# Delta rule: one of three modulation chunks as one-column products on TensorE, between the fills of the inverse's levels

## The chip, the core and the metric

One core of one Trainium2 chip. The metric is the time of one execution of the whole program on the device, in microseconds (us). The kernel before was run three times (2866.32, 2871.13 and 2872.02 us, median 2871.13); one more execution was recorded by the hardware profiler.

## What is computed

The reference is a stack of two transformer blocks at 256 tokens and a width of 2048. The change touches one stage of the first block, the gated delta rule, and a vector that this stage computes on the side:

```
mod = silu(c) @ w_ada + b_ada                       # 2048 x 12288, six parts of 2048 columns
...
m = strict_lower(beta * (k k^T) * gamma)            # per head and chunk of tokens
sol = triangular_solve(I + m, rhs)                  # u and w of the delta rule
v_new = u - w S ;  o = (q e^g) S + (q k^T * gamma) v_new ;  S = S * tail + k_tail^T v_new
```

`mod` is a product of a vector with a matrix of 2048 x 12288. Its weights are read once, in 24 chunks of 512 columns, and the chunks are spread as side work over several stages. The stage of the delta rule makes three of them (chunks 15, 16 and 17).

## The kernel before, in words

The stage is the function `phase_gdn`. All engines work at once, each in the order of its own code, and wait for each other by semaphores only. Eight heads are held in four quads of squares (n = 0 to 3), with 128 tokens to a square.

The triangular system is solved by building the inverse in levels. The code numbers them l = 0 to 5. In each level TensorE fills four banks `("p", l, n)` (8 products of 64x64 each), ScalarE copies each to `P1` (line 2127), TensorE fills four banks `("d", l, n)` (16 products of 64x64 each; the profile shows an f32 product as two records, so 16 records for a p and 32 for a d), and VectorE merges each into `T` and `UD` with two predicated copies (lines 2359 and 2361). The fill p of quad n of the next level waits until VectorE has merged d of quad n. TensorE has one queue: it makes p of the four quads, then d of the four quads, in this order. All fills are recorded at line 2164. The last level (l = 5) is half as large. Level 0 is followed by four `qk` banks.

After the last level VectorE copies the squares to `U` (lines 2381 and 2384), and TensorE goes on with the state products `vn0`, `s`, `ks`, `vn1` and the outputs. ScalarE's last steps (a logarithm, the load of a table, an exponential) end the stage.

The side work is the class `Ada`: POOL loads 512 KB of `w_ada` at a time (two rows of tiles of 128x512, line 233) into a ring of four slots, and VectorE multiplies each tile by one number per partition and adds it up (line 274 for the first two steps of a chunk, line 278 for the rest). Sixteen steps make a chunk, and three more operations reduce it (lines 283, 289 and 292); TensorE sums the rest over partitions after the outputs (line 191), and VectorE adds the bias (line 179). VectorE's code places the steps by two tables: `LEVEL_STEPS` says how many steps follow the merge of each quad in levels 0 to 4, and two more numbers how many stand before the keys and the outputs. What is left is done after the outputs.

SyncE issues nothing in this stage. `gdn_work` is a buffer of five parts; its last, `BB`, is free from the last `strict_products` of VectorE until ScalarE squares the outputs into it.

One-column products with weights as the stationary operand exist elsewhere in the program: in the setup stage `ada_group` makes two chunks so (line 344).

Of the kernel before, what the change touches and what calls it, by code (L numbers as in the profile page):

```python
# [14 lines left out]
P = 128  # L15
# [3 lines left out]
KT = D // P  # L19
# [7 lines left out]
CW = 512  # L27
NT = CW // P
# [132 lines left out]
AK = 2  # L161
# [3 lines left out]
AGROUPS = KT // AK  # L165
ADA_BANK = 7


def ada_column(which, chunk):

    return NMOD * which + NT * chunk


def add_bias(nc, core, which, chunk, chunks, bank=ADA_BANK):

    at, n = NT * chunk, NT * chunks
    bias = (C_BADA, C_BADA2)[which] + at
    sums = ada_column(which, chunk)
    return nc.vector.tensor_tensor(core.mod[:, which, at:at + n], core.ps[:, bank, sums:sums + n],
                                   core.cols[:, bias:bias + n], ALU.add)  # L180
# [1276 lines left out]
            next(program, None)  # L1457


GDN_CHUNKS = (15, 16, 17)  # L1460
LEVEL_STEPS = (2, 2, 2, 2, 2)
STEPS_BEFORE_KEYS, STEPS_BEFORE_OUTPUTS = 5, 2


AFTER_REFILL = {2: (2, 3), 3: (4,), 4: (5,), 5: (6, 7), 6: (8,), 7: (9,)}
# [538 lines left out]
def phase_gdn(nc, core, w_ada):  # L2004


    big, ps = core.big, core.ps
# [4 lines left out]
    NI = len(inv_levels)  # L2012
# [14 lines left out]
    with ExitStack() as ctx:  # L2027
# [3 lines left out]
        sem = lambda n: ctx.enter_context(nc.semaphore(n))  # L2031
        silu_ready, eg_ready, \
            g1_ready, g1_exp, nt_ready, tu_ready, r0_ready, eg_bc, qd_ready, sq_ready, \
            rs_ready, r1_ready, qkm_ready, cleared = (sem(n) for n in (
                "silu_gg_ready", "eg_ready", "g1_ready", "g1_exp", "nt_ready", "tu_ready", "r0_ready",
                "eg_bc", "qd_ready", "sq_ready", "rs_ready", "r1_ready", "qkm_ready", "inverse_cleared"))
        W = ctx.enter_context(nc.sbuf_tensor("gdn_work", [P, 5, HH * SEQ], F32))
        G1, QK, NT_, GB, BB = (W[:, n, :] for n in range(5))
        rows = ctx.enter_context(nc.sbuf_tensor("gdn_rows", [HH, 2, SEQ], F32))
# [13 lines left out]
        ident_square = ctx.enter_context(nc.sbuf_tensor("ident_square", [P, HP], F32))  # L2053
        ada = Ada(ctx, nc, core, [(w_ada, 0, chunk, 1) for chunk in GDN_CHUNKS], 1)
        block = ctx.enter_context(nc.Block())
# [5 lines left out]
        as_blocks = lambda a: a.rearrange("p (n t) -> p n t", t=P)  # L2061

        made = {}

        @block.gpsimd
        def _(pool):
# [8 lines left out]
            for n in reversed(range(1, len(LEVELS))):  # L2075
# [7 lines left out]
                if n in (4, 2):  # L2083
                    for load in range(4 + (4 - n), 6 + (4 - n)):
                        ada.load_when_free(pool, 0, load)
            for load in range(8, len(GDN_CHUNKS) * AGROUPS):
                ada.load_when_free(pool, 0, load)
# [71 lines left out]
        def _(pe):  # L2159
            def fill(name, parts):  # L2160

                banks.wait_empty(pe, name)
                for out, lhsT, rhs, start, stop in parts:
                    ins = nc.tensor.matmul(out, lhsT, rhs, start=start, stop=stop)
                ins.then_inc(banks.filled, 1)
# [20 lines left out]
            for j, (of, r, c) in enumerate(((gates, 0, 0), (gates, 0, 1), (gates, 1, 0), (gates, 1, 1), (rows, 0, 1),  # L2186
                                            (rows, 1, 0))):
                ins = nc.tensor.transpose(ps[:, banks.bank("columns"), j * HH:(j + 1) * HH],
                                          of[:, r, c * P:(c + 1) * P], core.ident[0:HH, 0:HH])
# [7 lines left out]
            def in_quad(n):  # L2197
                return [(j, 4 * n + j) for j in range(4)]

            for half in range(2):  # L2200
                for n in range(2 * half, 2 * half + 2):
                    pe.wait_ge(nt_ready, n + 1)
                    fill(("nt", n), [(half_ps(("nt", n), 0)[e, j, :], NTb[e, m, e], core.ident[e, e], True, True)
                                     for j, m in in_quad(n) for e in EDGES])
                for n in range(2 * half, 2 * half + 2):
                    fill_turned(("v", n), [big[:, GV + 2 * n + j // 2, (j % 2) * P:(j % 2 + 1) * P] for j in range(4)])
            for n in range(2):
                fill_turned(("kt", n), [big[:, GK + 4 * n + j, 0:P] for j in range(4)])
            for l in range(NI):
                for n in range(4):  # L2210
                    if l == 0:
                        pe.wait_ge(tu_ready, n + 1)
                    else:
                        pe.wait_ge(banks.emptied["dve"], n_dve[("d", l - 1, n)])
                    p = half_ps(("p", l, n), 0)
                    if l < NI - 1:
                        fill(("p", l, n), [(p[e, j, :], NTb[e, m, e], T[e, m, :], True, True)
                                           for j, m in in_quad(n) for e in EDGES])
                    else:
                        fill(("p", l, n), [(p[LOW, j, :], NTb[TOP, m, LOW], T[TOP, m, :], True, True)  # L2220
                                           for j, m in in_quad(n)])
                for n in range(4):
                    pe.wait_ge(banks.emptied["act"], n_act[("p", l, n)])
                    d, dt = half_ps(("d", l, n), 0), half_ps(("d", l, n), 1)
                    if l < NI - 1:
                        fill(("d", l, n), [(d[e, j, :], UD[e, m, :], P1[e, m, :], True, True)
                                           for j, m in in_quad(n) for e in EDGES]
                             + [(dt[e, j, :], P1[e, m, :], UD[e, m, :], True, True)
                                for j, m in in_quad(n) for e in EDGES])
                    else:  # L2230
                        fill(("d", l, n), [(dt[TOP, j, :], P1[LOW, m, :], UD[LOW, m, :], True, True)
                                           for j, m in in_quad(n)])
                if l == 0:
                    fill_products("qk", q_all, 0, 4)
# [38 lines left out]
        def _(dve):  # L2273
# [34 lines left out]
            def columns_of(a, L, high):  # L2308
                return a.rearrange("p n (b two l) -> p n b two l", two=2, l=L)[:, :, :, high, :]
# [27 lines left out]
            for n in range(4):  # L2337
# [3 lines left out]
                for edge in EDGES:  # L2341
                    ins = nc.vector.copy_predicated(columns_of(quad(UD, n)[edge], 1, 1),
                                                    mask_of(up_square, last, 1, 1, edge),
                                                    columns_of(quad(NTb, n)[edge, :, edge], 1, 1))
# [9 lines left out]
            for l, L in enumerate(inv_levels[:-1]):  # L2354
                m = LEVELS.index(L)
                dve.wait_ge(core.pool.sem, made[m])
                for n in range(4):
# [5 lines left out]
                                              ).then_inc(banks.emptied["dve"], 1)  # L2363
                    sum_steps(LEVEL_STEPS[l])
                if l == 0:
# [22 lines left out]
            for n in range(2):  # L2388
                banks.wait_filled(dve, ("ks", n))
                for j in range(4):  # L2390
                    h = 4 * n + j
                    ins = nc.vector.scalar_tensor_tensor(out=value(1, h), in0=quad_ps(("ks", n))[:, j, :],
                                                         scalar=pc[:, 6, h:h + 1], in1=value(1, h),
                                                         op0=ALU.mult, op1=ALU.add)
# [7 lines left out]
            for n, at in enumerate(quarters):  # L2402
# [3 lines left out]
                    in1=flat(GG, HH)[:, at], op0=ALU.mult, op1=ALU.mult).then_inc(banks.emptied["dve"], 1)  # L2406
            sum_steps(KT * len(GDN_CHUNKS) - done)
            for n, at in enumerate(quarters):
# [2 lines left out]
                v.mark(nc.vector.tensor_tensor(o[:, at], o[:, at], GB[:, at], ALU.mult))  # L2411
            dve.wait_ge(v.sem, v.n)
            ada.add_biases(dve)

# [1089 lines left out]
```

## Time and profile before

| | us |
|---|---|
| median of three runs | 2871.13 (2866.32 to 2872.02) |
| profiled execution, time | 2862.77 |
| its span, first to last instruction | 2861.0 |
| the stage of the delta rule in it | 556.4 to about 655.4 |
| levels 1 to 4 on TensorE | 589.15 to about 622 |

Times in the trace count from the first instruction. An engine's busy time in a window counts what it does, not whether anybody waits for it. PEclk, the granted clock, is 1.00 at 2.4 GHz and 0.50 at 1.2 GHz.

### The profile page before, as it was taken

The page shows a single profiled execution, that of the slowest core. Times are in us where ns is not written, and L with a number is a line of the kernel's source. Part 1 is how long each engine was busy: PE and PEld are TensorE (multiplying, and loading weights), DVE is VectorE, ACT ScalarE, POOL GpSimd, SP SyncE. Part 2 cuts the span into 40 slices and gives each one's busy share as a digit, 9 for nine tenths or more (in the row PEclk, how much of TensorE's full clock was granted, in tenths as well). Part 3 has the DMA queues.
Part 4 walks back from the last instruction along what each step waited for, and adds up shares of the span by engine and source line. Part 5 has one row for each costly group of instructions (what it writes and reads, how often), then busy time and mean ns, then how long its engine had stood idle before and what let it go on. Part 6 is the DMA issues. An engine that isn't in the chain of part 4 may idle for free. (4 is left out here: it accounts for less than half of the span.)

```text
span 2861.0 us, 50952 instructions
## 1 busy us (share of the span) xinstructions
PE 2726.7 (95%) x19637; PEld 2514.4 (88%) x19637; DVE 2038.9 (71%) x2921; ACT 1369.9 (48%) x2222; POOL 462.9 (16%) x592
## 2 busy tenths in 40 slices
PE   8799999988999999999998999998999999999998
PEld 8789999877878888999998988887878888889998
DVE  6768996786877777777877588785587655555554
ACT  1355446545455555445444454555344444444454
POOL 1002998121011111111110022220011000000000
PEclk7799999989999999999999999999999999999999
DMA  9756666546487887887883776664568655665563
GB/s 386 253 202 234 220 228 202 196 149 221 153 283 270 279 276 267 272 275 267 283 279 87 204 230 231 215 221 136 162 242 292 224 182 184 190 191 161 178 190 127
DMA packets 290940, 632.48 MB, mean 221 GB/s; under 512 B 31490, under 2 KB 52422, under 8 KB 290502
## 3 DMA queue, kind: packets, MB, share of 16 engines
q1 hardware_dynamic: 239120, 484.78, 51.0%
q0 software_dynamic: 40192, 142.63, 14.7%
q10 hardware_dynamic: 11446, 2.54, 0.6%
q8 instruction: 127, 2.08, 0.3%
q14 instruction: 55, 0.45, 0.0%
HBM read 627.77 MB, written 2.10 MB: 220 GB/s over the span
## 5 line engine op out<-in xcount | busy, mean ns | idle before, releaser
L1188 DVE TENSOR_TENSOR weight_parts<-weights,weight_parts 128x1024 fp32r<-128x1024 f32 x584 | 705.9, 1220 | 298.5 <-ACT weight_parts L1109 297.9
L1109 ACT ACTIVATE weight_parts<-weights 128x1024 fp32r<-128x1024 f32 x584 | 606.4, 1056 | 556.4 <-PE accumulators L1298 245.3
L1287 PE MATMUL accumulators<-h_parts,weight_parts 128*128 128x512 f32 x2816 | 780.7, 399 | 19.8 <-DVE h_parts L1175 8.5
L1287 PEld LDWEIGHTS accumulators<-h_parts,weight_parts 128*128 128x128 f32 x2816 | 487.3, 191 | 90.1 <-DVE h_parts L848 9.4
L1298 PEld LDWEIGHTS accumulators<-h_parts,weight_parts 128*128 128x128 f32 x2944 | 454.1, 191 | 68.5 <-DVE weight_parts L1188 7.5
L1298 PE MATMUL accumulators<-h_parts,weight_parts 128*128 128x256 f32 x2944 | 473.6, 283 | 5.6 <-DVE weight_parts L1188 5.6
L1333 PE MATMUL accumulators<-h_parts,weight_parts 128*128 128x256 f32 x1728 | 436.1, 284 | 1.8 <-DVE weight_parts L1188 1.8
L1335 PE MATMUL accumulators<-h_parts,weight_parts 128*128 128x256 f32 x1728 | 435.6, 284 | 0.0
L1333 PEld LDWEIGHTS accumulators<-h_parts,weight_parts 128*128 128x128 f32 x1728 | 333.9, 193 | 2.3 <-DVE weight_parts L1188 2.3
L1335 PEld LDWEIGHTS accumulators<-h_parts,weight_parts 128*128 128x128 f32 x1728 | 333.8, 193 | 0.0
L1329 PE MATMUL accumulators<-h_parts,weight_parts 128*128 128x256 f32 x1728 | 279.9, 285 | 8.9 <-ACT weight_parts L1109 8.9
L1655 PE MATMUL accumulators<-in_h_parts,in_weight_parts 128*128 128x256 f32 x1024 | 263.2, 289 | 13.9 <-DVE in_weight_parts L1976 13.6
L1657 PE MATMUL accumulators<-in_h_parts,in_weight_parts 128*128 128x256 f32 x1024 | 260.0, 286 | 0.0
L1815 ACT ACTIVATE in_weight_parts<-weights 128x512 fp32r<-128x512 f32 x256 | 157.2, 630 | 201.8 <-PE accumulators L1657 147.8
L1329 PEld LDWEIGHTS accumulators<-h_parts,weight_parts 128*128 128x128 f32 x1728 | 240.1, 193 | 9.3 <-ACT weight_parts L1109 9.3
L1976 DVE TENSOR_TENSOR in_weight_parts<-weights,in_weight_parts 128x512 fp32r<-128x512 f32 x256 | 188.4, 748 | 77.0 <-ACT in_weight_parts L1815 76.6
L2884 PE MATMUL accumulators<-in_h_parts,in_weight_parts 128*128 128x256 f32 x1632 | 216.8, 287 | 9.7 <-DVE in_weight_parts L3269 4.1
L2884 PEld LDWEIGHTS accumulators<-in_h_parts,in_weight_parts 128*128 128x128 f32 x1632 | 203.3, 192 | 21.0 <-issue 8.4
L1655 PEld LDWEIGHTS accumulators<-in_h_parts,in_weight_parts 128*128 128x128 f32 x1024 | 199.0, 194 | 19.0 <-DVE in_weight_parts L1976 18.7
L1657 PEld LDWEIGHTS accumulators<-in_h_parts,in_weight_parts 128*128 128x128 f32 x1024 | 199.3, 195 | 0.0
L3020 ACT ACTIVATE in_weight_parts<-weights 128x512 fp32r<-128x512 f32 (+6 forms) x224 | 120.8, 554 | 153.8 <-PE accumulators L2884 146.0
L1648 PE MATMUL accumulators<-in_h_parts,in_weight_parts 128*128 128x256 f32 x1024 | 177.0, 296 | 3.7 <-DVE in_h_parts L1846 3.7
(409 smaller groups left out, 3373.3 us busy)
## 6 DMA issues: line engine op xcount, KB each, us to landing
weights<-in_w_ff SPq DMA_DIRECT2D x256, 512.0 KB, 5.5
weights<-in_w_in SPq DMA_DIRECT2D x160, 512.0 KB, 5.0
h_t<-in_ada_w POOLq DMA_DIRECT2D x96, 512.0 KB, 6.6
weights<-in_ffn_w_gate SPq DMA_DIRECT2D x88, 512.0 KB, 4.6
weights<-in_ffn_w_up SPq DMA_DIRECT2D x88, 512.0 KB, 4.6
weights<-in_ffn_w_down SPq DMA_DIRECT2D x88, 512.0 KB, 4.2
weights<-in_w_out SPq DMA_DIRECT2D x64, 512.0 KB, 4.6
wide<-in_ada_w POOLq DMA_DIRECT2D x128, 256.0 KB, 3.8
```

The source lines that it names most:

```text
L1109: nc.scalar.activation(w[:, held:held + take, 0, :], core.ring[:, q % RING, k:k + take, :], ACT.Copy).then_inc(core.high_ready, take)
L1188: ins = nc.vector.tensor_tensor(w[:, held:held + take, 1, :], core.ring[:, q % RING, k:k + take, :], w[:, held:held + take, 0, :].bitcast( ...
L1287: nc.tensor.matmul(core.ps[:, nt, :], high, x[:, kt].rearrange("p a t -> p (a t)"), start=(kt == 0), stop=False, skip_group_check=True)
L1298: ins = nc.tensor.matmul(rest(nt) if two else acc(c, nt), w[:, held, 1, nt * P:(nt + 1) * P], x[:, kt, 0, :], start=False, stop=(kt == KT ...
L1329: nc.tensor.matmul(accs[nt], w[:, held, 0, cols[nt]], xk[:, 0, :], start=(first and nt % 2 == 0), stop=False, skip_group_check=True)
L1333: nc.tensor.matmul(accs[nt], w[:, held, 0, cols[nt]], xk[:, 1, :], start=False, stop=False, skip_group_check=True)
L1335: ins = nc.tensor.matmul(accs[nt], w[:, held, 1, cols[nt]], xk[:, 0, :], start=False, stop=(last and nt % 2 == 1), skip_group_check=True)
L1648: nc.tensor.matmul(acc(c, nt), w[:, k, 0, nt * P:(nt + 1) * P], x[:, kt, 0, :], start=(kt == 0 and nt % 2 == 0), stop=False, skip_group_ch ...
L1655: nc.tensor.matmul(acc(c, nt), w[:, k, 0, nt * P:(nt + 1) * P], x[:, kt, 1, :], start=False, stop=False, skip_group_check=True)
L1657: ins = nc.tensor.matmul(acc(c, nt), w[:, k, 1, nt * P:(nt + 1) * P], x[:, kt, 0, :], start=False, stop=(kt == KT - 1 and nt % 2 == 1), sk ...
L1976: ins = nc.vector.tensor_tensor(w[:, k, 1, :], core.ring[:, g % RING, part, :], w[:, k, 0, :].bitcast(F32), ALU.subtract)
L2884: ins = nc.tensor.matmul(out, stationary[:, a], moving[:, b], start=(kt == 0 and i == 0 and j == 0), stop=(kt == KT - 1 and i == 2 and j = ...
```

## The change

Chunk 17 leaves VectorE. Its 16 rows of tiles become 64 one-column products on TensorE: the stationary operand is a 128x128 square of weights, the moving one a column of `c_act`, and the sums stay in one PSUM bank until VectorE adds the bias. Two products follow each p fill and each d fill of levels 1 to 4 (32 places with two products each). SyncE loads the weights in eight loads of 512 KB into two slots in `BB`; a load waits until TensorE has used up the slot, and TensorE waits for a load at every fourth place. VectorE's tables shrink from 48 steps to 32: one step instead of two behind each merge of levels 2 to 4, two instead of five before the keys, one instead of two before the outputs.

```diff
-GDN_CHUNKS = (15, 16, 17)
-LEVEL_STEPS = (2, 2, 2, 2, 2)
-STEPS_BEFORE_KEYS, STEPS_BEFORE_OUTPUTS = 5, 2
+GDN_CHUNKS, GDN_PE_CHUNK = (15, 16), 17
+LEVEL_STEPS = (2, 2, 1, 1, 1)
+STEPS_BEFORE_KEYS, STEPS_BEFORE_OUTPUTS = 2, 1
...
+        mod_ring = BB.rearrange("p (s k n) -> p s k n", s=2, k=AK)
+
+        @block.sync
+        def _(sp):
+            sp.wait_ge(nt_ready, 4)
+            for load in range(AGROUPS):
+                if load >= 2:
+                    sp.wait_ge(mod_used, load - 1)
+                sp.dma_start(mod_ring[:, load % 2], mod_columns[:, load]).then_inc(mod_landed[load % 2], 16)
...
+            def modulation(point):
+                kt = point // 2
+                load = kt // AK
+                if point % (2 * AK) == 0:
+                    pe.wait_ge(mod_landed[load % 2], 16 * (load // 2 + 1))
+                for j in (2 * (point % 2), 2 * (point % 2) + 1):
+                    ins = nc.tensor.matmul(ps[:, ADA_BANK, mod_at + j:mod_at + j + 1],
+                                           mod_ring[:, load % 2, kt % AK, j * P:(j + 1) * P], core.c_act[:, kt:kt + 1],
+                                           start=(kt == 0 and j == 0), stop=(kt == KT - 1 and j == NT - 1),
+                                           skip_group_check=True)
+                if point % (2 * AK) == 2 * AK - 1:
+                    ins.then_inc(mod_used, 1)
...
+                    if 1 <= l < NI - 1:
+                        modulation(8 * (l - 1) + n)
...
+                        if l:
+                            modulation(8 * (l - 1) + 4 + n)
...
             ada.add_biases(dve)
+            dve.wait_ge(mod_used, AGROUPS)
+            add_bias(nc, core, 0, GDN_PE_CHUNK, 1)
```

On TensorE, level 1 and the start of level 2 stood so before. Rows `wide,gdn_work 64x64` are p fills, rows `wide 64x64` are d fills, and x32 is four fills of 8 products:

```order
L2164 MATMUL accumulators<-wide 128x128 x16
L2164 MATMUL accumulators<-wide,gdn_work 64x64 x32
L2164 MATMUL accumulators<-wide 64x64 x64
L2164 MATMUL accumulators<-wide,gdn_work 64x64 x32
L2164 MATMUL accumulators<-wide 64x64 x64
```

With the change, a part of the same level reads so; line 2176 is the fills and line 2218 the new products:

```order
L2176 MATMUL accumulators<-wide 128x128 x16
L2176 MATMUL accumulators<-wide,gdn_work 64x64 x8
L2218 MATMUL accumulators<-c_act,gdn_work 128x1 x2
L2176 MATMUL accumulators<-wide,gdn_work 64x64 x8
L2218 MATMUL accumulators<-c_act,gdn_work 128x1 x2
L2176 MATMUL accumulators<-wide,gdn_work 64x64 x8
L2218 MATMUL accumulators<-c_act,gdn_work 128x1 x2
L2176 MATMUL accumulators<-wide,gdn_work 64x64 x8
L2218 MATMUL accumulators<-c_act,gdn_work 128x1 x2
L2176 MATMUL accumulators<-wide 64x64 x16
L2218 MATMUL accumulators<-c_act,gdn_work 128x1 x2
```

Each of the 32 fills of levels 1 to 4 is now followed by a pair of products with the whole array as its tile, and the next fill stands behind that pair.

On VectorE, the piece from the last quad of level 3 through level 4 to the copies of `U` stood so before (lines 2359 and 2361 are a merge, 274 and 278 the steps of the side work):

```order
L2359 COPY_PREDICATED wide<-low_square,accumulators 128x8x16
L2361 COPY_PREDICATED wide<-up_square,accumulators 128x8x16
L278 SCALAR_TENSOR_TENSOR ada_sums<-ada_weights,c_act,ada_sums 128x512 x2
L283 TENSOR_TENSOR ada_sums<-ada_sums 128x512
L289 STREAM_TRANSPOSE ada_sums<-ada_sums 128x512
L292 TENSOR_REDUCE ada_rows<-ada_sums 128x16
L2359 COPY_PREDICATED wide<-low_square,accumulators 128x4x32
L2361 COPY_PREDICATED wide<-up_square,accumulators 128x4x32
L274 TENSOR_SCALAR ada_sums<-ada_weights,c_act 128x512 x2
L2359 COPY_PREDICATED wide<-low_square,accumulators 128x4x32
L2361 COPY_PREDICATED wide<-up_square,accumulators 128x4x32
```

With the change the same piece is (lines 2388 and 2390 are the merge):

```order
L2388 COPY_PREDICATED wide<-low_square,accumulators 128x8x16
L2390 COPY_PREDICATED wide<-up_square,accumulators 128x8x16
L278 SCALAR_TENSOR_TENSOR ada_sums<-ada_weights,c_act,ada_sums 128x512
L2388 COPY_PREDICATED wide<-low_square,accumulators 128x4x32
L2390 COPY_PREDICATED wide<-up_square,accumulators 128x4x32
L278 SCALAR_TENSOR_TENSOR ada_sums<-ada_weights,c_act,ada_sums 128x512
```

One step stands where two stood, and the reduction of a chunk between levels 3 and 4 is gone; the second chunk is now reduced behind the outputs, where the third was.

## Rows read from the trace of the kernel before

**Rows 1.** The page: busy time, share of the span and instructions.

```profile
PE 2726.7 (95%) x19637; PEld 2514.4 (88%) x19637; DVE 2038.9 (71%) x2921; ACT 1369.9 (48%) x2222; POOL 462.9 (16%) x592
```

**Rows 2.** Stretch: length; busy of PE, PEld, DVE, ACT, POOL; PEclk, DMA share, GB/s.

```profile
596.00:606.00 10.00, 6.40 (x197) 5.86 (x194) 9.90 (x20) 4.84 (x16) 3.24 (x5) 1.00 0.64 219
```

**Rows 3.** Timeline of VectorE, levels 2 to 5: start, length, instruction, idle time before.

```profile
601.88 2.28 DVE L2370 TENSOR_TENSOR gdn_work<-gdn_work,incl 128x2048 f32<-128x2048 f32 x1
...
619.19 0.69 DVE L283 TENSOR_TENSOR ada_sums<-ada_sums 128x512 f32<-128x512 f32 x1
...
621.26 0.29 DVE L2359 COPY_PREDICATED wide<-low_square,accumulators 128x128 f32<-128x128 int32 x1
...
626.29 1.41 DVE L278 SCALAR_TENSOR_TENSOR ada_sums<-ada_weights,c_act,ada_sums 128x512 f32<-128x512 f32 x2
627.61 2.40 DVE L2381 COPY wide<-wide 64x256 f32<-64x256 f32 x8
630.03 1.41 DVE L2384 COPY wide<-accumulators 64x256 f32<-64x256 f32 x4
631.47 3.40 DVE L278 SCALAR_TENSOR_TENSOR ada_sums<-ada_weights,c_act,ada_sums 128x512 f32<-128x512 f32 x5
637.45 2.40 DVE L2392 SCALAR_TENSOR_TENSOR wide<-accumulators,gdn_token_cols,wide 128x128 f32<-128x128 f32 x8 [2.58 <-PE accumulators L2164]
```

**Rows 4.** Timeline of TensorE, levels 1 and 2, and the first state product.

```profile
589.15 2.48 PE L2164 MATMUL accumulators<-wide,gdn_work 64*64 64x64 f32 x64
591.55 3.95 PE L2164 MATMUL accumulators<-wide 64*64 64x64 f32 x128
...
596.79 0.68 PE L2164 MATMUL accumulators<-wide,gdn_work 64*64 64x64 f32 x16 [0.36 <-DVE wide L2361]
...
607.53 1.12 PE L2164 MATMUL accumulators<-wide,gdn_work 64*64 64x64 f32 x16 [1.04 <-DVE wide L2361]
...
626.95 2.73 PE L2164 MATMUL accumulators<-wide 64*64 64x64 f32 x29
630.88 5.57 PE L2164 MATMUL accumulators<-wide 128*128 128x128 f32 x32 [1.20 <-issue]
```

**Rows 5.** Timeline of TensorE, windows 576.3:577 and 578.7:579.3 (cut at their edges).

```profile
576.12 0.57 PE L2164 MATMUL accumulators<-ident,gdn_work 64*64 64x64 f32 x14
576.63 0.55 PE L2170 MATMUL accumulators<-ident,wide 128*128 128x128 f32 x3
...
578.51 0.60 PE L2170 MATMUL accumulators<-ident,wide 128*128 128x128 f32 x4
579.04 0.45 PE L2164 MATMUL accumulators<-wide,gdn_work 64*64 64x64 f32 x8
```

**Rows 6.** Two groups of records: duration ns min/median/max, first and last start.

```profile
L2164 PE MATMUL accumulators<-wide,gdn_work x368: 218/218/366, 579.0 to 646.0; 64*64 64x64 f32 x176, 128*128 128x128 f32 x8
...
L2170 PE MATMUL accumulators<-ident,wide x24: 272/273/330, 574.3 to 578.8; 128*128 128x128 f32 x24
```

**Rows 7.** Timeline of TensorE in the setup stage, one-column products.

```profile
35.66 3.63 PE L344 MATMUL accumulators<-c_act,weights 128*128 128x1 f32 x32
...
74.77 6.96 PE L344 MATMUL accumulators<-c_act,weights 128*128 128x1 f32 x32
```

**Rows 8.** TensorE by stretch: length, busy time (records), granted clock, DMA share, GB/s.

```profile
40.40:53.90 13.50, 13.50 (x66) 0.50 1.05 405
...
603.00:607.10 4.10, 1.36 (x32) 1.00 0.30 108
607.50:610.10 2.60, 1.97 (x32) 0.50 0.73 203
610.10:613.90 3.80, 3.80 (x78) 0.50 0.89 319
```

**Rows 9.** DMA issues in the window 583:630.

```profile
ada_weights<-in_w_ada POOLq DMA_DIRECT2D x20, 512.0 KB, 4.9
```

**Rows 10.** Timeline of VectorE, the stage's last operation.

```profile
655.21 0.17 DVE L179 TENSOR_TENSOR modulation<-accumulators,small_vectors 128x12 f32<-128x12 f32 x1
```

More of the change, by code:

```diff
@@ L2033, in phase_gdn @@
             g1_ready, g1_exp, nt_ready, tu_ready, r0_ready, eg_bc, qd_ready, sq_ready, \
-            rs_ready, r1_ready, qkm_ready, cleared = (sem(n) for n in (
+            rs_ready, r1_ready, qkm_ready, cleared, mod_used, *mod_landed = (sem(n) for n in (
                 "silu_gg_ready", "eg_ready", "g1_ready", "g1_exp", "nt_ready", "tu_ready", "r0_ready",
-                "eg_bc", "qd_ready", "sq_ready", "rs_ready", "r1_ready", "qkm_ready", "inverse_cleared"))
+                "eg_bc", "qd_ready", "sq_ready", "rs_ready", "r1_ready", "qkm_ready", "inverse_cleared", "pe_modulation_used",
+                "pe_modulation_landed_0", "pe_modulation_landed_1"))
+        mod_columns = w_ada.rearrange("(g k p) n -> p g k n", p=P, k=AK)[:, :, :, GDN_PE_CHUNK * CW:(GDN_PE_CHUNK + 1) * CW]
+        mod_at = ada_column(0, GDN_PE_CHUNK)
         W = ctx.enter_context(nc.sbuf_tensor("gdn_work", [P, 5, HH * SEQ], F32))
```

## The prediction, made before the kernel was run

> **What bounds the kernel now.** I read the page first: TensorE is busy for 95% of the span and VectorE for 71% [rows 1]. That is a mean over many stages and says little of a change that sits in one of them, the stage of the delta rule, about 100 us long. So I went to that stage's windows and timelines. In 596 to 606 VectorE is busy for 9.90 of 10 us and TensorE for 6.40 [rows 2]. The timelines show who ends whose wait: inside levels 1 to 4 TensorE's gaps before a p fill end with VectorE's merge at line 2361 (0.36 and 1.04 us in [rows 4]), while VectorE goes from one row into the next, through the mask of QK (2.28 us), the steps and the reduction of a chunk [rows 3]. VectorE therefore sets the pace of levels 1 to 4, with side work between the merges. TensorE starts level 1 at 589.15, and the first state product starts at 630.88 [rows 4], right after VectorE's copies to U at 627.61 and 630.03 [rows 3]. From there TensorE and ScalarE set the end: VectorE waits 2.58 us for TensorE although it still had five steps of side work to fill the time [rows 3]. The number to forecast is when the first state product starts; what lies behind it moves with it.
>
> **What is taken from VectorE.** Levels 2 to 4 lose 12 steps. Two steps take 1.41 us from first start to last end, but a step overlaps the next, so one is worth about 0.67 us (five take 3.40, [rows 3]): 8.0 us. The reduction of a chunk from 619.19 to the next merge at 621.26 also goes from the levels: 2.1 us. Together 10.1 us on the engine that bounds now. The three steps fewer before the keys (2 us) and the one fewer before the outputs stand ahead of waits and bring nothing: the 2.58 us only grow.
>
> **What TensorE gets.** 64 products, seen as two records each, are 128 records. Setup shows such records back to back: 32 in 3.63 us at the full clock, 0.113 us each, and 32 in 6.96 us at half, 0.22 each [rows 7]. That makes 14.3 us at full clock. But they come as 32 groups of four records between fills whose tile is 64x64, and each group changes the tile twice. The trace has such changes. The last 64x64 record before 576.63 starts at 576.12 + 0.57 - 0.22 = 576.47, so entering costs 0.16 us; the third record of the 128x128 run starts 0.55 - 0.27 = 0.28 us after the first, the fourth 0.11 later, 0.39 in all; the way back is from 578.51 + 0.60 - 0.27 = 578.84 to 579.04, 0.20 us [rows 5, 6]. A group of four thus puts 0.16 + 0.39 + 0.20 = 0.75 us between two fills instead of 4 x 0.113 = 0.45. Those rows have 128 moving columns or few, mine have one; I take 0.75 and keep 0.45 as the lower bound, and for the upper the doubled figure at half clock. The Trainium skill ("TensorEngine Tiling (Array Packing)", Key Properties) says that a change of tiling mode drains the engine; the trace agrees with its 0.16 and 0.20 us, and without that rule the sum would go by 0.45.
>
> **A level on TensorE, full clock.** A p fill takes 0.68 - 0.22 = 0.46 us from first to last start [rows 4, 6], a d fill about 0.90 (four with their gaps take 3.95, [rows 4]). With a group behind each: 4 x (0.46 + 0.75) + 4 x (0.90 + 0.75) = 11.4 us. Four levels take 45.8 us from 589.15, so the last d fill of level 4 is in at 589.15 + 45.8 - 0.75 = 634.2. Before it was about 622, where VectorE was then some 4 us behind. VectorE no longer is: merge to 635.0, a step to 635.7, copies to U 2.40, first half of the next 0.7 [rows 3], and the first state product starts near 639, 8 us later than before. By the lower bound, 0.45 a group, fills and groups take 4 x (2.40 + 3.75 + 3.6) = 39.0 us, and the first state product starts 1.8 us later. VectorE's 10.1 us cannot be had because TensorE becomes the bound, and only its lag at the end, 4 us, comes back.
>
> **The clock.** This decides the size. In setup TensorE runs one-column products without a gap, 13.50 of 13.50 us busy, and the granted clock is 0.50 [rows 8]; the first such run, from 35.66, was still at the full rate [rows 7]. So these products do not hold the clock up there. Among the fills the clock fell to 0.50 at about 607, after 4.1 us in which TensorE made two p fills (32 records, 1.36 us busy). It stayed at 0.50 through 607.5 to 610.1, two more p fills, 12 records a us, and came back only behind d fills without a gap, 78 records in 3.8 us, 20 a us [rows 8]. With the change the p part of a level gives 16 fill records every 1.21 us, 13 a us, for nearly 5 us, with only one-column products between. I expect the clock to fall in the p fills of level 1, near 593.5. At half clock a p fill takes about 0.9 us (1.12 less one record, [rows 4]), a d fill 1.56 (78 records in 3.8 us, [rows 8]) and a group 1.5: 2.4 and 3.06 us, so 7 and 10 fill records a us. Both are sparser than the stretch that did not bring the clock back, so it stays at 1.2 GHz until the state products. A level is then 4 x 5.46 = 21.8 us, four are 87.4; the first 4.4 us at full clock save 4.4. The last d fill is in at 589.15 + 87.4 - 4.4 - 1.5 = 670.6. Level 5's fills wait behind the last group (1.5 us) and are 64 records of one tile at a time, about 0.1 us each (29 in 2.73, [rows 4]), 6.4 us. The first state product starts at about 678.6, 48 us later than before.
>
> **What costs nothing.** The loads: total bytes stay, eight of 512 KB move to a queue that is empty here. Such a load lands 4.9 us after issue [rows 9]. A slot is free for the length of the other part of a level, 4.8 or 6.6 us at full clock and twice that at half, so TensorE waits at most about 1 us a level at full clock (3 us in all, upper bound) and not at all at half. If that cover went, each load late would delay fills and merges alike. SyncE's next work is in the next stage. VectorE's extra bias addition is 0.17 us [rows 10] on the stage's end. The wait in front of it, for TensorE's last group, is long over.
>
> **The sum.** 48 + 0.2 us on the profiled execution's 2862.8 (span 2861.0 and 1.8 around it): 2911. The median of the runs is 8.3 us above that execution, so 2871.1 + 48 = 2919. For this forecast alone I give 2905 to 2926: fall of the clock one level part earlier or later, groups of 1.2 to 1.6 us.
>
> **Rivals.** (1) Full clock throughout, with the drain: TensorE becomes the bound, +8 us, 2879 (up to 2882 with load waits). For it: d fills with groups still give 32 records in 1.65 us, 19 a us, near the 20 of the stretch that restored the clock. Against it: the p parts, and setup. The Trainium skill ("TensorE: Matmul & The Clock Gate", The HAM clock gate) ties the grant to how busy the engine has been; taken as busy time, that is this rival, and the setup rows, fully busy at 0.50, are against it. (2) The clock falls only in level 3 or comes back for a while: two levels at 11.4 and two at 21.8, +27 us, 2898. (3) The products cost no more than in setup, without drain: +1.8 us, 2873, no difference that can be told. (4) The other side: weights are loaded under the running fills and the groups vanish in TensorE's gaps, so VectorE's 10.1 us come out. For a gain of 5.7 us (0.2%, about what a measurement of this kernel can tell from no change) the last d fill must be in by about 620, so a group may cost 6.4/31 = 0.2 us; break-even is at 0.39. If all of it hid, 10 us off: 2861. Setup's 0.113 us a record with nothing else running speaks against it, as the loads of weights already overlap there.
>
> **How the numbers follow.** Chances: half clock from level 1, 0.50; (2) 0.17; (1) 0.17; (3) 0.10; (4) 0.06. The predicted time is that of the first, 2919. The range 2875 to 2926 takes in (1), (2) and the first, less their tails, and leaves about 0.1 below and 0.06 above. Slower by over 0.2%: 0.84; within: 0.10; faster: 0.06.
>
> **What would show it.** In the profile after, VectorE should wait for TensorE before its merges in levels 1 to 4 instead of the other way round, most of all for d fills. Windows over levels 1 to 4 should show granted clock near 0.5 and TensorE busy almost without a gap; at full clock a level of 11 us means rival (1). The gaps around each group of four records show 0.16 and 0.20 us, or nothing, which is rival (3). The first state product's start gives the sum directly. The prediction is wrong if a group is much cheaper than 0.75 us, because p fills are then dense enough in time to keep the clock and the whole rest of the argument goes.

## The result, and the profile after

The changed kernel is slower: 2890.05 us in the median of 11 runs (2878.62 to 2901.83) against 2867.03 for 11 runs of the kernel before (2858.46 to 2872.02). The ratio is 1.0076, with a 95% interval of 1.0062 to 1.0090, so 22 us (18 to 26). On another chip it came out as 1.0092 (1.0064 to 1.0120). The direction was forecast, and so was a clock that falls and stays down, but at more than twice the size: 48 us. The runs of the changed kernel also lie 23 us apart, those of the kernel before 14.

The page of its profiled execution (2890.64 us), first rows, which answer to [rows 1]:

```profile
span 2888.9 us, 51183 instructions
PE 2757.4 (95%) x19765; PEld 2539.6 (88%) x19765; DVE 2031.9 (70%) x2903; ACT 1371.1 (47%) x2222; POOL 451.0 (16%) x584
```

TensorE has the 128 new records (19765 against 19637), and the shares are what they were. The page does not show where 28 us went. The timeline of TensorE does. First the start of level 1, then level 3, which has the change from one clock to the other in it, then level 4 (line 2176 is the fills, line 2218 the new products):

```profile
594.79 0.68 PE L2176 MATMUL accumulators<-wide,gdn_work 64*64 64x64 f32 x16
595.40 0.61 PE L2218 MATMUL accumulators<-c_act,gdn_work 128*128 128x1 f32 x4
595.93 0.68 PE L2176 MATMUL accumulators<-wide,gdn_work 64*64 64x64 f32 x16
596.54 0.61 PE L2218 MATMUL accumulators<-c_act,gdn_work 128*128 128x1 f32 x4
597.08 0.68 PE L2176 MATMUL accumulators<-wide,gdn_work 64*64 64x64 f32 x16
...
605.83 0.68 PE L2176 MATMUL accumulators<-wide,gdn_work 64*64 64x64 f32 x16
...
620.32 0.68 PE L2176 MATMUL accumulators<-wide,gdn_work 64*64 64x64 f32 x16
620.93 0.61 PE L2218 MATMUL accumulators<-c_act,gdn_work 128*128 128x1 f32 x4
621.47 1.89 PE L2176 MATMUL accumulators<-wide 64*64 64x64 f32 x32
...
632.75 1.12 PE L2176 MATMUL accumulators<-wide,gdn_work 64*64 64x64 f32 x16
633.79 1.01 PE L2218 MATMUL accumulators<-c_act,gdn_work 128*128 128x1 f32 x4
634.73 1.12 PE L2176 MATMUL accumulators<-wide,gdn_work 64*64 64x64 f32 x16
...
652.05 3.35 PE L2176 MATMUL accumulators<-wide,gdn_work 64*64 64x64 f32 x29
```

Level 1 takes 605.83 - 594.79 = 11.04 us without a gap, level 4 takes 652.05 - 632.75 = 19.3. Between them, in the d part of level 3, the length of a d fill goes from 1.15 to 1.97 us. The windows of TensorE (stretch, length, busy time and records, granted clock, DMA share, GB/s) say why:

```profile
594.80:605.80 11.00, 11.00 (x225) 1.00 0.64 212
605.80:616.90 11.10, 11.10 (x227) 1.00 0.79 275
616.90:621.50 4.60, 4.60 (x83) 1.00 0.82 271
621.50:632.70 11.20, 11.20 (x145) 0.50 0.36 109
632.70:652.00 19.30, 19.30 (x225) 0.50 0.17 56
```

The clock falls once and does not come back in the levels. TensorE is busy the whole time at either clock. The waits on VectorE and TensorE in the same stretch, the kernel before first (589 to 631), then the changed kernel (594 to 665):

```profile
PE accumulators L2164 <- DVE wide L2361: 8.4, 10, 1.7
```

```profile
DVE wide L2388 <- PE accumulators L2176: 29.1, 12, 9.7
```

Before, TensorE waited 8.4 us for VectorE's merges; now VectorE waits 29.1 us for TensorE's fills, and TensorE waits for nobody in this stretch, not for a load either.

As a milestone for all kernels I take VectorE's first row after the levels that needs TensorE's state products, the update of the values by the keys. In the changed kernel it is

```profile
665.43 2.40 DVE L2421 SCALAR_TENSOR_TENSOR wide<-accumulators,gdn_token_cols,wide 128x128 f32<-128x128 f32 x8 [4.76 <-PE accumulators L2176]
```

70.6 us after level 1 starts (594.79). Before it was 637.45 - 589.15 = 48.3 us [rows 3, 4]. So 22.3 of the 27.9 us between the two spans arise here. Another 3.9 lie ahead of level 1, where TensorE runs the same code in both kernels: the stage starts at 556.41 and 558.15, and level 1 follows 32.7 and 36.6 us later. In the changed kernel's profile TensorE ran at clock 0.50 from 560 to 580, in the other for about half of that time. The windows of 560 to 580, kernel before first:

```profile
560.00:580.00 20.00, 19.36 (x147) 0.76 0.26 96
```

```profile
560.00:580.00 20.00, 19.93 (x67) 0.50 0.31 106
```

This part took 32.7 us in e8, the changed kernel again, so it is scatter and not the change. In what follows "milestone" is the time from the start of level 1 to that row of VectorE.

The milestone has 32 records of state products in it, and before they ran at half clock for the most part:

```profile
631.00:634.40 3.40, 3.40 (x16) 0.50 0.24 99
```

They took 5.57 us [rows 4], where the same records at full clock take 3.87 (e1, below). So the milestone of the kernel before is about 1.6 us late by its clock alone. Where that matters I give the start of the first state product as well, which is what the prediction forecast. It came 41.7 us after level 1 starts before and 63.9 in the changed kernel (at 658.70), 22.2 us later.

### The profile page after: what moved, and what is told of

The parts are those of the page before. It is cut to its first block and busy times, and to the rows that moved or that the text cites. A ratio compares the mean times of both kernels' runs of the same rounds, so it can differ in the third digit from the quotient of the medians.

```text
span 2888.9 us, 51183 instructions
## 1 busy us (share of the span) xinstructions
PE 2757.4 (95%) x19765; PEld 2539.6 (88%) x19765; DVE 2031.9 (70%) x2903; ACT 1371.1 (47%) x2222; POOL 451.0 (16%) x584
## 5 line engine op out<-in xcount | busy, mean ns | idle before, releaser
L1298 PEld LDWEIGHTS accumulators<-h_parts,weight_parts 128*128 128x128 f32 x2944 | 453.2, 190 | 71.2 <-DVE weight_parts L1188 10.3
```

Of the source, the lines that this page charges most:

```text
L1298: ins = nc.tensor.matmul(rest(nt) if two else acc(c, nt), w[:, held, 1, nt * P:(nt + 1) * P], x[:, kt, 0, :], start=False, stop=(kt == KT ...
```

## Experiments

All ratios are against runs of the kernel before on the same chip, with 6 to 12 runs of each kernel; g2 is a single run. A milestone comes from the one profiled run of its kernel.

| kernel | ratio (95%) | milestone, us |
|---|---|---|
| before | 1 | 48.3 |
| changed | 1.0076 (1.0062 to 1.0090) | 70.6 |
| e1, no products | 0.9953 (0.9936 to 0.9970) | 40.1 |
| e2, products on top | 1.0090 (1.0065 to 1.0114) | 70.7 |
| e3, 96 moving columns | 1.0021 (1.0004 to 1.0038) | 55.5 |
| e4, grouped | 1.0015 (0.9999 to 1.0030) | 52.7 |
| e5, grouped, 96 columns | 1.0009 (0.9997 to 1.0021) | 49.5 |
| e6, quarters | 1.0032 (1.0018 to 1.0046) | 53.0 |
| e7, all behind d | 1.0040 (1.0022 to 1.0059) | 60.3 |
| e8, changed again | 1.0092 (1.0064 to 1.0120) | 79.4 |
| g1, all behind p | 1.0048 (1.0031 to 1.0064) | 60.7 |
| f1, grouped, 96 columns, two groups at the stage's end | 0.9989 (0.9974 to 1.0005) | 45.4 |
| f2, the same with one column | 1.0001 (0.9987 to 1.0016) | 48.5 |
| g2, changed, third profile | one run | 63.3 |

The theory has two parts: TensorE becomes the bound of the levels, and its clock falls because one-column products stream next to nothing.

**e1: no products at all.** Both calls of `modulation` and SyncE's loads are taken out, so chunk 17 is not computed.

```diff
-                    if 1 <= l < NI - 1:
-                        modulation(8 * (l - 1) + n)
...
-                        if l:
-                            modulation(8 * (l - 1) + 4 + n)
```

> Chunk 17 is left out altogether: no products on TensorE, no loads by SyncE, its four columns of the modulation hold the bias alone; VectorE has the thinner tables of the changed kernel. Theory (the products and their changes of tile on TensorE are the whole loss, and VectorE's relief of 10 us is real): the first state product starts some 8 to 10 us earlier than before, TensorE's fills take about 25 us at full clock, and the time is 7 to 10 us under before (ratio near 0.997). Rival (VectorE's side work was hidden anyway, or the stage is held by something else in the new order): same as before, ratio 1.000.

It was 13 us faster (9 to 18), at 2853.98 us, where 7 to 10 were expected. TensorE's first state products:

```profile
626.88 3.87 PE L2168 MATMUL accumulators<-wide 128*128 128x128 f32 x32 [1.23 <-issue]
```

They start 35.2 us after level 1 (591.68), 6.5 us earlier than before and not the 8 to 10 expected. The milestone is 8.2 us earlier; the other 1.6 us are the state products at full clock instead of half. So VectorE's relief is real, if less than the 10.1 us taken from it, and the products are the whole loss. About 4 of the 9.8 us between the two profiled spans arise behind the milestone, in code that both kernels share; these are not explained, nor is the rest up to the median of 13.

**e2: the products on top of VectorE's three chunks.**

```diff
-GDN_CHUNKS, GDN_PE_CHUNK = (15, 16), 17
-LEVEL_STEPS = (2, 2, 1, 1, 1)
-STEPS_BEFORE_KEYS, STEPS_BEFORE_OUTPUTS = 2, 1
+GDN_CHUNKS, GDN_PE_CHUNK = (15, 16, 17), 17
+LEVEL_STEPS = (2, 2, 2, 2, 2)
+STEPS_BEFORE_KEYS, STEPS_BEFORE_OUTPUTS = 5, 2
```

The products write columns of another PSUM bank, `WARM_BANK`, that nobody reads.

> VectorE makes all three chunks as before, and TensorE makes chunk 17 once more into columns that nobody reads. Theory (TensorE is the bound with the products in it, so the relief of VectorE is worth only its lag at the end): 2 to 5 us above the changed kernel, 12 to 30 us above before depending on how long the clock is at half. Rival (the relief of 10 us is had in full beside the products): 10 us above the changed kernel, 32 us above before.

Here the clock happened to fall 26.9 us after the start of level 1, and 26.8 us in the changed kernel, so the two profiles can be laid side by side. This is e2's milestone row; level 1 starts at 596.94:

```profile
667.59 2.40 DVE L2421 SCALAR_TENSOR_TENSOR wide<-accumulators,gdn_token_cols,wide 128x128 f32<-128x128 f32 x8 [2.81 <-PE accumulators L2176]
```

It stands 70.65 us behind, against 70.64. With the products in, taking 10 us of work off VectorE moves nothing at all up to here in these two profiles. I had allowed it 2 to 5 us. The times can't tell: 1.0090 and 1.0076, on two chips, have overlapping intervals. The rival, 10 us above the changed kernel, is out.

**e3: 96 moving columns instead of one.**

```diff
-                    ins = nc.tensor.matmul(ps[:, ADA_BANK, mod_at + j:mod_at + j + 1],
-                                           mod_ring[:, load % 2, kt % AK, j * P:(j + 1) * P], core.c_act[:, kt:kt + 1],
+                    ins = nc.tensor.matmul(ps[:, WARM_BANK, P + 96 * j:P + 96 * j + 96],
+                                           mod_ring[:, load % 2, kt % AK, j * P:(j + 1) * P],
+                                           core.c_act[:, kt:kt + 1].to_broadcast([P, 96]),
```

The bias is added to column 0 of each 96. The sums stand in `WARM_BANK`, as in e2, and the last filler product of the stage, which writes the same bank, signals VectorE.

> The changed kernel, but each product streams the same column of c_act 96 times instead of once, into a bank of its own; the 128x128 rows of the stage with 128 moving columns pace at 0.11 us a record as the one-column ones do, so the products take no longer. Theory (the clock falls because one-column products stream next to nothing): the granted clock stays at 1.00 through levels 1 to 4 in the trace, all runs lie close together, 8 to 12 us above before (ratio 1.003 to 1.004). Rival (the clock falls because of the gaps at the changes of tile, or the stage's fills alone): the same falls as in the changed kernel, ratio near 1.0076 and runs 20 us apart.

This separates the two parts of the theory. Its windows over levels 1 to 4, and its first state products (window 639.8 to 643.4):

```profile
589.30:601.00 11.70, 11.70 (x227) 1.00 0.63 207
601.00:612.60 11.60, 11.60 (x225) 1.00 0.77 257
612.60:624.30 11.70, 11.70 (x225) 1.00 0.59 174
624.30:636.00 11.70, 11.70 (x226) 1.00 0.36 123
```

```profile
639.82 3.76 PE L2176 MATMUL accumulators<-wide 128*128 128x128 f32 x31
```

The number of records, their places and the changes of tile are those of the changed kernel; a group is 0.08 us longer, and the clock stays at 1.00. What is left is the bound alone: the first state product starts 50.5 us after level 1 (589.28), 8.8 us later than before, the milestone is 7.2 us later, and the ratio is 1.0021 (1 to 11 us) instead of 1.0076; 8 to 12 us were expected. The changes of tile are the same here, so they alone do not make the clock fall. Nor does the bank: e2 has its one-column products in the same one, and its clock fell. It is not only the one profile, either. The mean granted clock of a whole run was 0.969 to 0.977 in the 12 runs of e3, and 0.960 to 0.968 in all 24 of the changed kernel and e2. The expectation of narrow scatter failed: the runs lie 23 us apart all the same (2861.42 to 2884.50), so not all of the scatter comes from this stretch.

**e4: 8 groups of 16 records instead of 32 of 4.**

```diff
-                    if 1 <= l < NI - 1:
-                        modulation(8 * (l - 1) + n)
+                    if 1 <= l < NI - 1 and n == 3:
+                        for point in range(4):
+                            modulation(8 * (l - 1) + point)
```

and the same for the d fills.

> The 8 products that stand behind the four p fills of a level come together behind the last of them, and likewise for d: 8 groups of 16 records instead of 32 of 4, so 24 changes of tile each way less. Theory (a change of tile each way costs about 0.24 us beside the records' own 0.112): 4 to 6 us less than the changed kernel at the same clock, with the clock still falling in some runs: 5 to 25 us above before, ratio 1.003 to 1.007. Rival (the changes cost nothing, the records all): no difference from the changed kernel, 1.0076.

TensorE's timeline of level 2, and the start of level 3:

```profile
597.64 2.08 PE L2176 MATMUL accumulators<-wide,gdn_work 64*64 64x64 f32 x64
599.65 1.95 PE L2218 MATMUL accumulators<-c_act,gdn_work 128*128 128x1 f32 x16
601.53 3.95 PE L2176 MATMUL accumulators<-wide 64*64 64x64 f32 x128
605.41 1.95 PE L2218 MATMUL accumulators<-c_act,gdn_work 128*128 128x1 f32 x16
607.28 2.08 PE L2176 MATMUL accumulators<-wide,gdn_work 64*64 64x64 f32 x64
```

A level takes 607.28 - 597.64 = 9.64 us, 1.40 less than with 32 groups; six changes of tile each way fewer, 0.23 us for one there and back. Both numbers are as worked out, 5.6 us in four levels. In its profile the clock fell only behind the levels (630.9), in level 5. The time, 1.0015, is less than the 1.003 to 1.007 expected and can hardly be told from before.

**e5: both edits.** The calls as in e4, the operand as in e3.

> Both edits at once: 96 moving columns a product and 8 groups of 16 records. Theory: full clock and 24 changes of tile less: the first state product some 3 to 5 us later than before, ratio 1.001 to 1.002. Rival (either edit does nothing): 8 to 23 us above before.

The first state product starts 44.5 us after level 1, 2.8 us later than before (3 to 5 were expected), the milestone is 1.2 us later, and the ratio is 1.0009, not to be told from e4's or from before. The clock is at 1.00 in all four levels, and eight changes of tile are left, about 8 x 0.23 = 1.8 us. TensorE is busy for 40.08 of the 40.80 us of the levels, so it is still the bound.

**e6: quarters.** Each product in four of 64x64, with the two halves of the sum in different banks.

```diff
+                    for turn in range(2):
+                        for e, f in ((EDGES[0], EDGES[turn]), (EDGES[1], EDGES[1 - turn])):
+                            ins = nc.tensor.matmul(out_of(e, f, j),
+                                                   mod_ring[e, load % 2, kt % AK, j * P + f.start:j * P + f.stop],
+                                                   core.c_act[e, kt:kt + 1],
```

> Each 128x128 product is cut into four of 64x64 on the same tiles as the fills, so the tile never changes in levels 1 to 4: 16 records behind each fill instead of 4. If two of them run side by side as in the fills (0.029 us a record) a group costs 0.47 us. Theory (the change of tile is 0.2 us or more of the 0.69 a group takes in the changed kernel): a fill and its group take 0.2 us less, 6 to 7 us in all, 3 us above before at full clock, up to 15 with the clock at half. Rival (no cost of the change of tile; or the quarters don't run side by side): as slow as the changed kernel or slower.

A fill with its group became much shorter than I expected. TensorE in level 1, the first records of the p fills of quads 0 to 2:

```profile
591.10 0.62 PE L2176 MATMUL accumulators<-wide,gdn_work 64*64 64x64 f32 x14
...
591.82 0.60 PE L2176 MATMUL accumulators<-wide,gdn_work 64*64 64x64 f32 x14
...
592.52 0.60 PE L2176 MATMUL accumulators<-wide,gdn_work 64*64 64x64 f32 x14
```

That is 0.71 us a p fill and group, against 1.15. But the time came to 1.0032, not better than e4. TensorE stood still, and the clock was at 0.50 for 13.6 us of the levels. TensorE's waits in 591 to 639, first those before a fill, and one of VectorE's:

```profile
PE accumulators L2176 <- issue: 5.3, 4, 2.7
PE accumulators L2224 <- issue: 1.0, 1, 1.0
PE accumulators L2224 <- DMA gdn_work<-in_w_ada: 0.5, 1, 0.5
DVE wide L2397 <- PE accumulators L2176: 15.1, 9, 4.1
```

"issue" means that the profile shows nothing that TensorE waited for. Three of the four such waits, 4.7 of the 5.3 us, begin in the middle of a fill (the longest behind the first records of a p fill, at 598.93), where the code has no wait for anybody. So it is not VectorE that held TensorE up there; VectorE itself waited 15.1 us for TensorE. The cause of these waits is open. The edit changes the tile, the size of a load of weights and what runs side by side, all at once, so it says that the groups can be cheap, not by which of the three.

**e7 and g1: where the groups stand.** In e7 each d fill has four products behind it and the p fills none; in g1 it is the other way round. The edit of e7:

```diff
-                    if 1 <= l < NI - 1:
-                        modulation(8 * (l - 1) + n)
...
-                            modulation(8 * (l - 1) + 4 + n)
+                            modulation(8 * (l - 1) + 2 * n)
+                            modulation(8 * (l - 1) + 2 * n + 1)
```

> All products stand behind the d fills, four behind each, none behind the p fills: 16 groups of 8 records. Theory: 16 changes of tile less, 3 to 4 us less than the changed kernel at full clock; TensorE waits now and then for VectorE before a p fill. The clock, which fell at the end of the p fills of level 3 in the changed kernel, may fall in the d part now. Ratio 1.002 to 1.007.

> All products stand behind the p fills, four behind each, none behind the d fills: 16 groups of 8 records, as many as in the kernel that has them all behind d. Theory (the clock falls where fills are sparsest, and stays down as long as groups keep following): the p part of level 1 has 16 fill records in 1.6 us, so the clock falls in or right behind the p part of level 1 or 2 in every profile, comes back in the d parts that are free of products, and the time lies above that of the kernel with all behind d: ratio 1.005 to 1.009 against its 1.004. Rival (only the number of records and changes of tile counts): 1.004, as with all behind d.

e7 gave 1.0040, g1 1.0048, with overlapping intervals and milestones of 60.3 and 60.7. The clock did fall behind the p parts in g1 (at 597.1, 607.3, 621.0 and 634.6) and came back in the d parts, as I said, but in e7 it fell too, at 610.8 and 627.9, in the d parts. The place alone is worth nothing that can be told; the rival holds. Both are faster than the changed kernel by their medians, though g1's interval (to 1.0064) still touches that of the changed kernel (from 1.0062). They have 16 changes of tile there and back fewer, 3.7 us at 0.23, and in both the clock came back between two falls, in fills without groups. How much of the gain each gives is not shown.

**e8 and g2: the changed kernel again.**

> The changed kernel once more, on the chip of the last three: ratio 1.0076 again, with runs spread over 20 us as before. Theory: the runs' time goes with the mean granted clock (0.968 in the fastest, 0.961 in the slowest so far).

> The changed kernel once more, for a third place at which the clock falls. It fell in the d part of level 3 (621.6) in one profile and in the p part of level 2 (604.2) in the other, and the first state product started 63.9 and 72.9 us after level 1. Theory: again a single fall, behind p fills, and no return before the state products; each level behind it takes 19.3 us instead of 11.0.

Windows of the two, e8 first, from the start of level 1:

```profile
589.40:600.50 11.10, 11.10 (x228) 1.00 0.63 210
600.50:604.10 3.60, 3.60 (x65) 1.00 0.86 277
604.10:616.80 12.70, 12.70 (x163) 0.50 0.52 186
```

```profile
615.10:626.20 11.10, 11.10 (x226) 1.00 0.62 189
626.20:629.80 3.60, 3.60 (x64) 1.00 0.84 254
629.80:643.30 13.50, 13.50 (x167) 0.50 0.12 44
```

In e8 the clock falls at the end of the p part of level 2 (604.2), in g2 at that of level 4 (629.9), in the first profile behind that of level 3 (621.6). The milestones are 79.4, 63.3 and 70.6. Each time, and in e2 too, it fell at the end of a row of p fills and groups, or right behind it, and it stayed down until TensorE was at the state products. g2 ran for 2882.03 us, with the before of its chip at 2866.17; e8's profiled execution took 2894.35. The mean clock of the first 11 runs goes with their times: 0.968 in the three fastest (2878.62 to 2881.80), 0.961 in the slowest (2901.83). Behind the fall a level takes 19.3 us in e8 as well.

**f1 and f2: a version from the findings.** Six groups of 16 stay in levels 1 to 3. The last two loads go to `NT_` once level 5's p fills have read it, and their products take the place of the filler products at the stage's end.

```diff
+                if load == 6:
+                    sp.wait_ge(banks.filled, banks.at[("p", NI - 1, 3)] + 1)
...
+            for point in range(24, 32):
+                modulation(point)
             ada.sum_rows(pe)
-            keep_warm(nc, core, pe, 8)
```

> Eight groups of 16 records with 96 moving columns, of which six stand in levels 1 to 3 and two behind the last squares of the stage, where TensorE has nothing but filler products for 8 us; their two loads go to the part of the buffer that the fills of level 5 have left. The filler products are gone. Theory (TensorE bounds the levels; what leaves them is gained until VectorE bounds again, at 35 us without any products): the first state product starts 38 to 41 us after level 1 starts, 3 to 5 us sooner than with all eight groups in the levels, and the time is 0 to 4 us under before (ratio 0.9985 to 1.000). Rival (the products behind the squares push out the stage's end): as the grouped and wide kernel, 1.0009, or slower.

> The same with one moving column instead of 96. Theory: the same places, but the clock is no longer held up by the products, so it falls in some runs behind groups of 16 records: 1 to 6 us slower than with 96 columns, 0 to 6 us above before. Rival (six groups in dense levels are too few to let the clock fall): equal to the kernel with 96 columns.

TensorE at the end of the stage in f1:

```profile
644.57 3.60 PE L2178 MATMUL accumulators<-gdn_work,ones 128*128 128x512 f32 x8
648.01 3.71 PE L2220 MATMUL accumulators<-c_act,gdn_work 128*128 128x96 f32 x32
651.65 0.25 PE L191 MATMUL accumulators<-ada_rows,fold 128*32 128x8 f32 x8
```

The fold at line 191 comes 2.6 us later behind the milestone than before, but the filler products behind it are gone, and VectorE's last addition of the stage stands 17.8 us behind the milestone in both kernels: the 32 records cost nothing there. The first state product starts 40.4 us after level 1 (38 to 41 were expected), and the milestone is 2.9 us earlier than before. The ratio of f1 is 0.9989 (0.9974 to 1.0005), a median of 2861.59 us against 2864.45; f2 has 1.0001. In f1's profile the clock is at 1.00 up to the milestone; in f2's it fell twice in the levels, at 592.1 and 619.4, for 3.4 us each, and the milestone is 3.1 us later than f1's. That is as expected, though the intervals of the two times overlap. By its milestone f1 is about 8 us ahead of the changed kernel at full clock (45.4 against about 53, e3's 55.5 less 2.5 for its longer groups), but neither is shown to beat the kernel before.

## Why the prediction was right and wrong

The prediction gave 2919 us; 2890.05 was measured. That is inside its wide range and nearest to its second rival (2898). What decides the size is when the clock falls, and that step failed.

**What bounds.** Right. e1 shows that VectorE bounded the levels before (the first state product comes 6.5 us earlier without the steps), e2 that with the products it is TensorE, and the waits in the profile turned round.

**The price of a group.** Right, a little high: 0.75 us stood in the sum. The changed kernel takes 4.59 us for the four p fills of level 1 and their groups (594.79 to 599.38), 1.15 each, of which 0.46 are the fill, so 0.69. A level at full clock was 11.04 us for 11.4. Of the 0.69 us, 0.24 are more than four records at their own pace (0.45), where the prediction had 0.30; e4 gives 0.23 for one change of tile there and back. The Trainium skill ("TensorEngine Tiling (Array Packing)", Key Properties) says that a change of tiling mode drains the engine; both numbers agree with it.

**Full clock throughout.** The first rival's +8 us holds. e3, whose groups are 0.08 us longer, has the first state product 8.8 us later than before; 32 x 0.08 = 2.5 us less would be about 6.3 for the one-column groups, an estimate.

**That the clock falls and stays down.** Right. The falls go with the one moving column as far as the runs show: in e3 the records, their places and the changes of tile are the same, and the clock stayed at 1.00. The profiles of the other kernels agree. With 96 columns (e3, e5, f1) it did not fall up to the milestone; with one column it fell in the levels in all but e4. It is not the products alone: in the kernel before it fell twice in this stretch without any.

**Where it falls.** This step failed. The prediction had the clock fall "in the p fills of level 1, near 593.5". It held through level 1 and level 2 in the first profile and in e2, through level 1 in e8 and through three levels in g2. The prediction read the stretch before the fall at 607 (two p fills in 4.1 us) and setup as if any stretch much sparser than dense d fills would do. The profiles show that 16 fill records and a group every 1.15 us come before a fall in one level and leave the clock up in another. So the rival with a fall in level 3 was the case of the first profile (22.2 us at the first state product), and the predicted case, a fall at once, was in no profile of the changed kernel. Where in the levels it falls differs from run to run, and that is part of the scatter. What decides the level in which it falls is not shown.

**A level at half clock.** Mis-sized. 21.8 us stood in the sum, 19.3 were measured. A p fill with its group takes 1.98 us (632.75 to 634.73), for 2.4: the group was doubled to 1.5 us, but takes 1.98 less 0.9, about 1.1. Even with the fall 4.4 us into level 1 the loss would have been about 39 us, by this estimate: e8's fall came 14.7 us in and cost 31.1, and 10.3 us more of the work at half clock cost 10.3 x (19.3/11.04 - 1) = 7.7. The place of the fall is thus the larger error (39 against 22), and the size of a level adds 9 (48 against 39).

**Two sums in the rivals.** By the prediction's own terms two levels at half clock with level 5 behind them give about 31 us, not the 27 of the second rival. And the lower bound takes 2.40 us for the four p fills of a level where the main sum has 4 x 0.46 = 1.84. Neither changes the forecast.

**The rest.** Loads hidden: right, TensorE waits for none. VectorE's steps before the keys worth nothing: right, the milestone's row waits for TensorE in every profile. VectorE's lag at the end given back: right at full clock. From the end of the last d fill of level 4 to the first state product it was 8.7 us before and is 4.4 in e3.

## What to carry to other kernels

Work that is moved from the engine that bounds to one with gaps costs its length there plus what it does to its neighbours: here 14 us of one-column products came with about 7.5 us of changes of tile (32 at 0.23 to 0.24), between fills whose gaps added up to 8. Put such products together rather than spread (e4), and where the engine has nothing else to do (f1). And look at the granted clock of an earlier stretch with the same kind of instruction before giving TensorE thin products. Being busy did not keep its clock up: it was busy for 19.30 of 19.30 us in level 4, at 0.50. With 96 columns instead of one, at nearly the same length, the clock stayed at 1.00 in all three profiles.

## What the runs showed of the hardware that was not expected

A product with 96 moving columns costs almost what one with a single column does: 16 records take 2.02 us (e5) against 1.95 (e4) from first start to last end. At half clock a group of four records takes 1.6 times as long as at full clock (about 1.1 us for 0.69), not twice. And 16 records of 64x1 behind a fill of the same tile take 0.25 us (0.71 less 0.46), about 0.016 each, where a 128x1 record takes 0.11.
